# A routed feed-forward's bias b1: added by a matmul on TensorE instead of copied to all partitions and added on VectorE

## The chip, the cores and the metric

One core of one Trainium2 chip. The metric is the time of one execution on the device in microseconds (us), as the median of several runs. Beside it stands one execution taken by the hardware profiler.

## The reference

One layer of an encoder over 512 tokens and 16 meta tokens of width 1024: an mLSTM branch and a latent attention branch, mixed by gates, and then a mixture of experts. The change lies in the last:

```python
def moe(x, w_router, b_router, w1, b1, w2, b2):
    logits = (xt @ w_router) + b_router
    top_val, top_idx = lax.top_k(logits, 4)          # 4 of 32 experts
    gates = jax.nn.softmax(top_val, axis=-1)
    ...
    def expert_block(args):
        toks, wts, e = args
        hid = x_pad[toks] @ w1[e] + b1[e]             # w1: 1024 x 2048, b1: 2048, f32
        glu = jnp.minimum(hid[..., :1024], 7.0)
        lin = jnp.clip(hid[..., 1024:], -7.0, 7.0)
        act = glu * jax.nn.sigmoid(1.702 * glu) * (lin + 1)
        return (act @ w2[e] + b2[e]) * wts[:, None]   # w2: 1024 x 1024
```

The outputs are summed for each token, added to the residual, and normalised.

## The kernel before

The five engines run programs of their own, joined by semaphores. The stages follow one another: projections and the mLSTM (TensorE's loop at line 1221, one pair of heads an iteration), attention (line 1269), gates and output projection (line 1324, until some 900 us), the router (to some 970), and then 32 experts, the larger part of the time.

An expert has room for 96 tokens, three tiles of 32. Its tokens' rows are gathered from DRAM by POOL, turned by TensorE (`turn_x`) and copied by ACT to `xgT`. `up` multiplies them by w1: for each of 8 chunks of 128 rows, 3 tiles by 4 quarters make 12 matmuls of 128x32 weights and 512 columns. Quarter j of the output goes to partitions 32 j to 32 j + 31 of PSUM bank t, so four matmuls work in four column groups of the array. DVE (`activate`) adds b1, clamps, and forms the activation with ACT's sigmoid; `turn_act` turns it, and `down` multiplies it by w2, 8 x 12 matmuls of 256 columns. POOL adds the rows to the result in DRAM.

TensorE's order is written out in `step(e)`: up of expert e, with turn_act(e - 1) and turn_x(e + 1) before its fifth chunk, then down of expert e - 1. Its loop (line 1436) holds two steps an iteration and has 15 iterations; expert 0's up, and the products with b2 (line 1433), stand ahead of it, and the last step and the last down behind it. The waits of a step are those of `step` and `up_start` (lines 1380 and 363), and one for each chunk (line 1387, with its value from line 1384).

The weights have 12 places of 1 MB in `ring`. SP's queue loads each again for the next expert as soon as TensorE has used it (`load_up`, `load_down`), so a chunk is loaded about one expert ahead of its use. The expert's row of b1 is copied to the partitions by four DMAs of 64 KB behind chunk 0, in two buffers in turn.

Of the kernel before, what the change touches and what calls it, by code (L numbers as in the profile page):

```python
# [50 lines left out]

K_ID, K_ONE, K_MF, K_MB, K_US, K_IO, K_EPS, K_HALF, K_QTR, K_END = 0, 128, 256, 384, 512, 640, 672, 673, 674, 676


def constant_tables():

    c = np.zeros((P, K_END), np.float32)
    s, t = np.arange(P)[:, None], np.arange(P)[None, :]
    c[:, K_ID:K_ID + P] = s == t
    c[:, K_ONE:K_ONE + P] = 1  # L60
    c[:, K_MF:K_MF + P] = np.where(s <= t, 0.0, NEG)
    c[:, K_MB:K_MB + P] = np.where(s >= t, 0.0, NEG)
    c[:, K_US:K_US + P] = s < t
    c[:, K_IO:K_IO + E] = np.arange(E)
    c[:, K_EPS] = EPS
    c[:, K_HALF] = -0.5
    c[:, K_QTR] = np.arange(P) // 32
    half = ROPE // 2
    freqs = np.float32(10000.0) ** (-np.arange(half, dtype=np.float32) / np.float32(half))
    pos = np.concatenate([np.arange(META, TK), np.arange(META)]).astype(np.float32)  # L70
    ang = (pos[None, :] * freqs.astype(np.float32)[:, None]).astype(np.float32)
    cos, sin = np.cos(ang).astype(np.float32), np.sin(ang).astype(np.float32)
    rope = np.stack([np.tile(cos, (4, 1)), np.concatenate([-sin, sin, -sin, sin])], 1)
    pair = np.zeros((P, MT, TOPK, 2), np.float32)
    pair[:, :, :, 0] = (np.arange(P)[:, None] + P * np.arange(MT)[None, :])[:, :, None]
    spare = np.zeros((32, NQ, E, 2), np.float32)
    spare[:, :, :, 0] = T + np.arange(32)[:, None, None] + 32 * (np.arange(NQ) % TT)[None, :, None]
    return {"c_table": c, "c_rope": np.ascontiguousarray(rope), "c_pair": pair.reshape(P, -1),
            "c_spare": spare.reshape(32, -1)}
# [36 lines left out]
def build(ctx, nc, x, meta, norm_mix, w_in, m_b_i, m_b_f, m_norm, w_m_proj, w_uq, w_ukv, a_norm_q,  # L116
# [48 lines left out]
    def col(*dims):  # L165
# [58 lines left out]
    w_r_sb = sb("w_r_sb", KT * E)  # L224
    b1_sb = sb("b1_sb", 4 * QR)
    b1_bc = [view(b1_sb, n * 2 * QR, 2, QR) for n in range(2)]
    ints = sb("ints", 192, I32)
# [14 lines left out]
    zeros_ready, spare_zeroed = sem("zeros_ready"), sem("spare_zeroed")  # L242
    gains_in, wr_in, xt_ready, xt_stored, pe_xt, xtT_ready, pe_lg = map(sem, (
        "gains_in", "wr_in", "xt_ready", "xt_stored", "pe_xt", "xtT_ready", "pe_lg"))
    ex_in, ex_ready, sel_ready, pe_pos, rows_ready, table_ready, spare_in, placed, tab_in, idx4_ready = map(sem, (
        "ex_in", "ex_ready", "sel_ready", "pe_pos", "rows_ready", "table_ready", "spare_in", "placed", "tab_in", "idx4_ready"))
    g_all_ready, pe_gT, gT_ready, pe_b2, b2_added, acc_in = map(sem, ("g_all_ready", "pe_gT", "gT_ready", "pe_b2", "b2_added", "acc_in"))
    chunk_in = [sem(f"chunk_in{c}") for c in range(SLOTS)]
    xg_in, y_out, b1_in = [[sem(f"{name}{n}") for n in range(2)] for name in ("xg_in", "y_out", "b1_in")]
    idx_ready, pe_tx, xgT_ready, w1_used, w2_used, pe_hid, hid_used = map(sem, (  # L250
# [91 lines left out]
    l_sb = view(low_sb, 0, TT, QR)  # L342
    b1_cols = b1.rearrange("e (c j n) -> e c j n", c=2, j=4)
    CHUNK_SLOT = [0, 1, 2, 3, 8, 9, 10, 11, 4, 5, 6, 7]
# [28 lines left out]
    def _(sp):  # L373
# [60 lines left out]

        def load_b1(n, e):

            for j in range(4):
                sp.dma_start(b1_bc[n][32 * j:32 * j + 32], b1_cols[bass.ds(e, 1), :, j, :].rearrange("e c n -> (e c) n").partition_broadcast(32)).then_inc(b1_in[n], 16)

        def load_up(i, n, e):  # L440

            for k in range(KT):
                if k < KT - 1:
                    sp.wait_ge(w1_used, i * (KT - 1) + (k + 2 - KT))
                else:
                    sp.wait_ge(pe_hid, i)
                load_w1(k, e)
                if k == 0:
                    load_b1(n, e)

# [9 lines left out]
        for k in range(KT):  # L460
            load_w1(k, 0)
        load_b1(0, 0)
        sp.wait_ge(pe_h, 2 * MT)
        for c in range(4):
            load_w2(c, 0)
        load_up(1, 1, 1)
        with sp.Fori(1, E // 2) as i:
            for n in range(2):
                load_up(i * 2 + n, n, i * 2 + n)
                load_down(i * 2 + (n - 1), i * 2 + (n - 1))  # L470
        load_down(E - 1, E - 1)
        over = overflow(sp)
        with sp.If(over > 0):
            with sp.Fori(0, over) as n:
                sp.wait_ge(y_out[0], n * 48 + 24 * E)
                expert = sp.value_load(over_i[0:1, bass.ds(n, 1)], min_val=0, max_val=E - 1)
                first = sp.value_load(over_i[0:1, bass.ds(n + OVW, 1)], min_val=0, max_val=NQ - TT)
                for j in range(4):
                    sp.dma_start(tab_ov[32 * j:32 * j + 32], tab_by[:, bass.ds(first, TT), bass.ds(expert, 1), :].rearrange("p q e v -> p q (e v)")).then_inc(tabo_in, 16)
                load_up(n + E, 0, expert)  # L480
                load_down(n + E, expert)
# [11 lines left out]
    def _(pool):  # L493
# [69 lines left out]
        pool.dma_start(tab_by.rearrange("p q e v -> p (q e v)"), c_spare).then_inc(spare_in, 16)  # L563
        pool.wait_ge(ao_ready, H + 1)
        pool.dma_start(b2_sb[0:E, :], b2).then_inc(wr_in, 16)
        for m in range(MT):
# [85 lines left out]
    def _(act):  # L652
# [129 lines left out]
        def y_rows(e, n, stored):  # L782
# [3 lines left out]
            nc.scalar.copy(y_sb[n], PS[:, 3:3 + TT, 0:QR]).then_inc(y_ready, 1)  # L786

        act.sem_inc(y_ready, 1)
        turned_x(0, 0)
        turned_x(1, 1)  # L790
# [4 lines left out]
        for e in range(2):  # L795
            turned_act(e)
            turned_x(e + 2, e)
            sigmoid(e + 1)
            y_rows(e, e, None)
        with act.Fori(1, E // 2 - 1) as i:  # L800
            for n in range(2):
                turned_act(i * 2 + n)
                turned_x(i * 2 + (2 + n), n)
                sigmoid(i * 2 + (1 + n))
                y_rows(i * 2 + n, n, i * 48)
# [6 lines left out]
        with act.If(over > 0):  # L812
            with act.Fori(0, over) as n:
                turned_x(n + E, 0)
                sigmoid(n + E)
                turned_act(n + E)
                y_rows(n + E, 0, n * 48 + 24 * E)
# [6 lines left out]
    def _(dve):  # L824
# [305 lines left out]

        def activate(e, n, biases, gates):
            st = Steps(dve, expert_steps, e * 3)
            bias = [b1_bc[n][:, c, :].unsqueeze(1).broadcast_to([P, TT, QR]) for c in range(2)]
            dve.wait_ge(b1_in[n], biases)
            dve.wait_ge(pe_hid, e + 1)
            st.did(V.tensor_tensor(g_sb, PS[:, 0:TT, 0:QR], bias[0], ALU.add))  # L1136
            V.tensor_tensor(l_sb, PS[:, 0:TT, QR:2 * QR], bias[1], ALU.add).then_inc(hid_used, 1)
            st.settle()
            V.tensor_scalar(g_sb, g_sb, 7.0, None, ALU.min).then_inc(g_ready, 1)  # L1139
            dve.wait_ge(hid_used, e + 1)  # L1140
            st.alone(V.tensor_scalar(l_sb, l_sb, -7.0, 7.0, ALU.max, ALU.min))
            dve.wait_ge(g_ready, e + 1)
# [5 lines left out]

        activate(0, 0, 64, lambda t: tab[:, t, 0, 1:2])
        for m in range(MT):  # L1150
            dve.wait_ge(pe_b2, m + 1)
            b = 3 + 2 * (m % 2)
            V.tensor_tensor(xs[:, m, :], xs[:, m, :], PS[:, b:b + 2, :].rearrange("p a b -> p (a b)"), ALU.add).then_inc(b2_added, 1)
        activate(1, 1, 64, lambda t: tab[:, t, 1, 1:2])
        with dve.Fori(1, E // 2) as i:
            for n in range(2):
                activate(i * 2 + n, n, i * 64 + 64, lambda t: tab[:, t, bass.ds(i * 2 + n, 1), 1])
        over = overflow(dve)
        with dve.If(over > 0):
            with dve.Fori(0, over) as n:  # L1160
                dve.wait_ge(tabo_in, n * 64 + 64)
                V.tensor_scalar(idx_ov, tab_ov[:, :, 0], 4.0, ct[:, K_QTR:K_QTR + 1], ALU.mult, ALU.add).then_inc(idx_ov_ready, 1)
                activate(n + E, 0, n * 64 + (32 * E + 64), lambda t: tab_ov[:, t, 1:2])

# [5 lines left out]
    def _(pe):  # L1170
# [207 lines left out]

        def up_start(e):
            pe.wait_ge(xgT_ready, e * 2 + 2)  # L1380
            passed(pe)

        def up(e, n, k):
            pe.wait_ge(chunk_in[k], e * 16 + 16)
            for t in range(TT):
                for j in range(4):
                    last = nc.tensor.matmul(PS[32 * j:32 * j + 32, t, :].rearrange("p (c n) -> p c n", c=2), xgT[n][:, k, 32 * t:32 * t + 32],  # L1387
                                            w1_c[k][:, :, j * QR:(j + 1) * QR], start=k == 0, stop=k == KT - 1)
            last.then_inc(pe_hid if k == KT - 1 else w1_used, 1)
# [16 lines left out]
        def step(e, n, gathers):  # L1406

            pe.wait_ge(hid_used, e)
            up_start(e)
            for k in range(KT):  # L1410
# [10 lines left out]
        turn_x(0, 0, 48)  # L1421
        up_start(0)
        for k in range(KT):
# [19 lines left out]
        with pe.If(over > 0):  # L1443
            with pe.Fori(0, over) as n:
                pe.wait_ge(y_ready, n + (E + 1))
                pe.wait_ge(hid_used, n + E)
                turn_x(n + E, 0, n * 48 + (24 * E + 48))
                up_start(n + E)
                for k in range(KT):
# [24 lines left out]
```

## Time and profile before

| | us |
|---|---|
| median of 3 runs | 2201.04 |
| the runs | 2199.01, 2201.04, 2213.47 |
| the profiled execution | 2208.45 |
| its span in the profile | 2206.7 |
| TensorE busy (matmul) | 1975.7 |
| VectorE, ScalarE, GpSimd busy | 444.3, 267.3, 331.8 |

The span is the time from the first to the last instruction that the profiler recorded; 1.75 us of the profiled execution lie around it. PE is TensorE's matmul and PEld its loading of weights, PEldq its sequencer; DVE is VectorE, ACT ScalarE, POOL GpSimd, SP SyncE. "Issue" is time in which an engine waited for nothing that the profile shows.

### The profile page before, as it was taken

To read this page: it belongs to the slowest core of one execution; us is meant where nothing else is said; L and a number is where in the kernel's file an instruction comes from. 1 tells how busy PE (TensorE), PEld (TensorE's weight loads), DVE (VectorE), ACT (ScalarE), POOL (GpSimd) and SP (SyncE) were. 2 spreads that over 40 slices of the span, in tenths; PEclk is the share of its full clock that TensorE was granted. 3 is DMA by queue.
4 is the path that set the end of the run, shared out by engine and by line. 5 is a ranking of instruction groups with operands and counts; after the bars stand their busy time and mean duration, and the time that the engine had idled before them with its cause. 6 is when DMAs were issued, how large, how long until landed. Compare 5 with 4: busy or idle time off the path is not lost.

```text
span 2206.7 us, 36817 instructions
## 1 busy us (share of the span) xinstructions
PE 1975.7 (90%) x15441; PEld 900.2 (41%) x15441; DVE 444.3 (20%) x899; ACT 267.3 (12%) x531; POOL 331.8 (15%) x387
## 2 busy tenths in 40 slices
PE   7898999899999999839898889888988998899894
PEld 5454555444444444513343334333333333343342
DVE  3333433433310000222010111001110101010111
ACT  2202201122210000100010001000000000100001
POOL 3000000000000000150212121222112221212112
PEclk8989999999999999868999999999999999999997
DMA  3302111002032224327999999999999999999995
GB/s 106 94 23 76 57 35 34 12 12 56 0 109 77 77 78 180 115 100 306 360 390 342 368 360 384 349 361 379 370 365 348 386 352 363 357 393 334 370 331 168
DMA packets 163598, 495.08 MB, mean 224 GB/s; under 512 B 16048, under 2 KB 88848, under 8 KB 130656
## 3 DMA queue, kind: packets, MB, share of 16 engines
q1 hardware_dynamic: 112064, 442.83, 52.6%
q0 software_dynamic: 21600, 32.83, 6.7%
q10 hardware_dynamic: 29776, 16.91, 2.7%
q8 instruction: 148, 2.42, 0.4%
q14 instruction: 10, 0.08, 0.0%
HBM read 472.71 MB, written 19.96 MB: 223 GB/s over the span
## 4 chain that ended last, share of the span: by engine, by line
PE 88%; issue 6%; DVE 2%; DMA 2%; POOL 2%; ACT 1%; SPq 0%; POOLq 0%; DVEq 0%; ACTq 0%
PE PS L357 35%; PE PS L1387 32%; PE PS L1399 15%; PE PS L1243 1%; PE PS L1376 1%; PE PS L1369 1%; DMA ring<-in_w_in 1%; PE PS L1320 1%; POOL tab_dram L579 1%; PE PS L1433 0%; DVE ring L959 0%; DMA x_sb<-acc_dram 0%; ACT at_sb L707 0%; PE PS L1345 0%; POOL small L542 0%
## 5 line engine op out<-in xcount | busy, mean ns | idle before, releaser
L1387 PE MATMUL PS<-ring,mix_sb 128*32 128x512 f32 x6144 | 721.9, 614 | 94.9 <-issue 92.4
L1387 PEld LDWEIGHTS PS<-ring,mix_sb 128*32 128x32 f32 x6144 | 200.2, 112 | 577.5 <-issue 574.7
L1399 PE MATMUL PS<-ring,hm_sb 128*32 128x256 f32 x6144 | 337.4, 379 | 0.9 <-ACT hm_sb L775 0.9
L357 PE MATMUL PS<-uT_sb,ring 128*128 128x512 f32 (+1 forms) x736 | 298.0, 561 | 6.5 <-DMA ring<-in_w_in 3.5
L1399 PEld LDWEIGHTS PS<-ring,hm_sb 128*32 128x32 f32 x6144 | 199.6, 110 | 146.0 <-issue 18.5
L1136 DVE TENSOR_TENSOR hm_sb<-PS,b_sb 128x768 f32<-128x768 f32 x32 | 30.6, 957 | 1019.5 <-PE PS L1387 1019.5
L357 PEld LDWEIGHTS PS<-uT_sb,ring 128*128 128x128 f32 x736 | 140.1, 209 | 158.6 <-issue 154.7
L598 POOL DMA_INDIRECT acc_dram<-hm_sb,ints x96 | 152.0, 1583 | 47.3 <-POOL ints L617 24.0
L357 PE MATMUL PS<-ring 128*128 128x129 f32 (+4 forms) x592 | 145.7, 377 | 6.8 <-DVE ring L1009 3.5
L617 POOL COPY ints<-ints 128x3 int32 (+1 forms) x32 | 5.9, 185 | 857.4 <-ACT hm_sb L786 857.4
L357 PEld LDWEIGHTS PS<-ring 128*128 128x128 f32 (+1 forms) x592 | 83.1, 193 | 65.4 <-issue 52.0
L592 POOL DMA_INDIRECT mix_sb<-xt_dram,ints x96 | 94.7, 986 | 47.2 <-POOL ints L606 24.9
L357 PE MATMUL PS<-low_sb,ring 64*128 64x512 f32 (+1 forms) x224 | 87.7, 503 | 7.3 <-DVE hm_sb L836 4.6
L775 ACT COPY hm_sb<-PS 128x384 f32<-128x384 f32 x64 | 28.9, 481 | 467.5 <-PE PS L1376 437.8
L780 ACT ACTIVATE hm_sb<-hm_sb 128x768 f32<-128x768 f32 x32 | 27.1, 847 | 376.5 <-DVE hm_sb L1139 376.5
L357 PE MATMUL PS<-ring,uT_sb 128*128 128x256 f32 (+1 forms) x320 | 70.5, 380 | 0.0
L357 PEld LDWEIGHTS PS<-ring,uT_sb 128*128 128x128 f32 (+1 forms) x320 | 54.2, 171 | 14.4 <-issue 1.3
L357 PEld LDWEIGHTS PS<-low_sb,ring 64*128 64x128 f32 (+1 forms) x224 | 37.1, 191 | 55.9 <-issue 49.9
L1369 PE MATMUL PS<-ct,mix_sb 128*128 128x128 f32 x192 | 26.9, 278 | 35.2 <-DMA mix_sb<-xt_dram,ints 35.2
L357 PE MATMUL PS<-ring,mix_sb 128*128 128x512 f32 x128 | 55.2, 593 | 1.6 <-DVE mix_sb L1040 1.6
L357 PE MATMUL PS<-hm_sb,ring 128*128 128x512 f32 x128 | 56.2, 592 | 0.0
L357 PE MATMUL PS<-at_sb,ring 128*128 128x512 f32 x128 | 56.2, 592 | 0.0
(240 smaller groups left out, 1114.6 us busy)
## 6 DMA issues: line engine op xcount, KB each, us to landing
ring<-in_w SPq DMA_DIRECT2D x384, 1024.0 KB, 7.9
ring<-in_w_in SPq DMA_DIRECT2D x8, 1024.0 KB, 5.2
b_sb<-in_b SPq DMA_DIRECT2D x128, 64.0 KB, 4.8
ring<-in_w_in ACTq DMA_DIRECT2D x14, 512.0 KB, 4.0
ring<-in_w_in SPq DMA_DIRECT2D x10, 512.0 KB, 5.2
ring<-m_dram POOLq DMA_DIRECT2D x16, 256.0 KB, 4.5
ring<-in_w_out SPq DMA_DIRECT2D x1, 4096.0 KB, 13.9
ring<-in_w_m_proj ACTq DMA_DIRECT2D x7, 512.0 KB, 3.8
```

The lines of the kernel that those rows point to most:

```text
L357: last = nc.tensor.matmul(out, w, r, start=n == 0, stop=n == len(pairs) - 1)
L579: pool.indirect_dma_start(out=tab_dram, out_offset=bass.IndirectOffsetOnAxis(ap=drow_i[:, n:n + 1], axis=0), in_=pair[:, m, k, :], in_offs ...
L592: pool.indirect_dma_start(out=xg[n][:, t, :], out_offset=None, in_=xt_dram, in_offset=bass.IndirectOffsetOnAxis(ap=idx[:, t:t + 1], axis=0 ...
L598: pool.indirect_dma_start(out=acc_dram, out_offset=bass.IndirectOffsetOnAxis(ap=idx[:, t:t + 1], axis=0), in_=y_sb[n][:, t, :], in_offset= ...
L775: nc.scalar.copy(actT.rearrange("p (j h) (t c) -> p h t j c", h=2, t=TT)[:, h], bank(6 + h)[:, 0:TT * P].rearrange("p (t j c) -> p t j c", ...
L780: nc.scalar.activation(s_sb, g_sb, ACT.Sigmoid, scale=1.702).then_inc(s_ready, 1)
L1136: st.did(V.tensor_tensor(g_sb, PS[:, 0:TT, 0:QR], bias[0], ALU.add))
L1243: nc.tensor.matmul(PS[0:r, 5 + n % 2, :], kT[h0:h0 + DQK, j * P:j * P + r], qT[h0:h0 + DQK, :], start=True, stop=True).then_inc(pe_s, 1)
L1320: nc.tensor.transpose(PS[:, 4 + k % 2, j * P:(j + 1) * P], pr[:, k % 3, j * P:(j + 1) * P], ident)
L1369: last = nc.tensor.transpose(PS[:, 3 + h, t * P:(t + 1) * P], xg[n][:, t, h * P:(h + 1) * P], ident)
L1387: last = nc.tensor.matmul(PS[32 * j:32 * j + 32, t, :].rearrange("p (c n) -> p c n", c=2), xgT[n][:, k, 32 * t:32 * t + 32], w1_c[k][:, :, ...
L1399: last = nc.tensor.matmul(PS[32 * j:32 * j + 32, 3 + t, 0:QR], actT[:, k, 32 * t:32 * t + 32], w2_c[k // 2][:, k % 2, j * QR:(j + 1) * QR] ...
```

## The change

b1 is loaded once, as 32 rows of 2048 f32, and POOL splits it into three bf16 parts whose sum is b1 to about 24 bits: the value rounded, the rest rounded, and the rest of that. They are held in `b1_part`, expert e's parts in partitions e, 32 + e and 64 + e; partitions 96 to 127 are zero. For each expert ACT copies one column of the constants, which is one in those three partitions and zero in the others, to a 128x32 bf16 tile, `b1_sel`. Before the first chunk of an expert TensorE multiplies it by `b1_part`: twelve matmuls over all 128 rows, which leave b1's row in each of the output's rows, and the chunks are added to that. DVE's adds are gone, and the two clamps read PSUM. The four DMAs an expert, their buffers and their semaphores are gone; SP's and DVE's loops now take one expert an iteration.

```diff
-K_ID, K_ONE, K_MF, K_MB, K_US, K_IO, K_EPS, K_HALF, K_QTR, K_END = 0, 128, 256, 384, 512, 640, 672, 673, 674, 676
+K_ID, K_ONE, K_MF, K_MB, K_US, K_IO, K_EPS, K_HALF, K_QTR, K_SEL, K_END = 0, 128, 256, 384, 512, 640, 672, 673, 674, 676, 708
...
+    c[0:96, K_SEL:K_SEL + E] = np.arange(96)[:, None] % 32 == np.arange(E)
...
-    b1_sb = sb("b1_sb", 4 * QR)
-    b1_bc = [view(b1_sb, n * 2 * QR, 2, QR) for n in range(2)]
+    b1_part = sb("b1_part", 2 * FF, BF16)
+    b1_low = sb("b1_low", 2 * FF, BF16, E)
+    b1_sel = [sb(f"b1_sel{n}", 32, BF16) for n in range(2)]
...
-    b1_cols = b1.rearrange("e (c j n) -> e c j n", c=2, j=4)
+    b1_f = view(low_sb, 0, 2 * FF)
+    b1_by = b1_part.rearrange("p (c n) -> p c n", c=2)
...
-        def load_b1(n, e):
-
-            for j in range(4):
-                sp.dma_start(b1_bc[n][32 * j:32 * j + 32], b1_cols[bass.ds(e, 1), :, j, :].rearrange("e c n -> (e c) n").partition_broadcast(32)).then_inc(b1_in[n], 16)
-
-        def load_up(i, n, e):
+        def load_up(i, e):
...
                 load_w1(k, e)
-                if k == 0:
-                    load_b1(n, e)
...
         pool.wait_ge(ao_ready, H + 1)
+        pool.dma_start(b1_f[0:E, :], b1).then_inc(b1f_in, 16)
+        st.alone(nc.gpsimd.memset(b1_part[:, :], 0.0))
+        pool.wait_ge(b1f_in, 16)
+        for n in range(3):
+            st.alone(nc.gpsimd.tensor_copy(b1_low[:, :], b1_f[0:E, :]))
+            nc.gpsimd.tensor_copy(b1_part[32 * n:32 * n + E, :], b1_low[:, :]).then_inc(b1_ready, 1)
+            if n < 2:
+                st.alone(nc.gpsimd.tensor_tensor(b1_f[0:E, :], b1_f[0:E, :], b1_low[:, :], ALU.subtract))
+        pool.wait_ge(b1_ready, 3)
         pool.dma_start(b2_sb[0:E, :], b2).then_inc(wr_in, 16)
...
+        def select(n, column):
+
+            nc.scalar.copy(b1_sel[n][:, :], column.broadcast_to([P, 32])).then_inc(b1_selected, 1)
+
         act.sem_inc(y_ready, 1)
+        for e in range(2):
+            select(e, ct[:, K_SEL + e:K_SEL + e + 1])
...
                 turned_x(i * 2 + (2 + n), n)
+                select(n, ct[:, bass.ds(i * 2 + (K_SEL + 2 + n), 1)])
                 sigmoid(i * 2 + (1 + n))
...
-        def activate(e, n, biases, gates):
-            st = Steps(dve, expert_steps, e * 3)
-            bias = [b1_bc[n][:, c, :].unsqueeze(1).broadcast_to([P, TT, QR]) for c in range(2)]
-            dve.wait_ge(b1_in[n], biases)
+        def activate(e, gates):
+            st = Steps(dve, expert_steps, e)
             dve.wait_ge(pe_hid, e + 1)
-            st.did(V.tensor_tensor(g_sb, PS[:, 0:TT, 0:QR], bias[0], ALU.add))
-            V.tensor_tensor(l_sb, PS[:, 0:TT, QR:2 * QR], bias[1], ALU.add).then_inc(hid_used, 1)
-            st.settle()
-            V.tensor_scalar(g_sb, g_sb, 7.0, None, ALU.min).then_inc(g_ready, 1)
+            V.tensor_scalar(g_sb, PS[:, 0:TT, 0:QR], 7.0, None, ALU.min).then_inc(g_ready, 1)
+            V.tensor_scalar(l_sb, PS[:, 0:TT, QR:2 * QR], -7.0, 7.0, ALU.max, ALU.min).then_inc(hid_used, 1)
             dve.wait_ge(hid_used, e + 1)
-            st.alone(V.tensor_scalar(l_sb, l_sb, -7.0, 7.0, ALU.max, ALU.min))
...
-        def up_start(e):
+        def up_start(e, n):
             pe.wait_ge(xgT_ready, e * 2 + 2)
+            pe.wait_ge(b1_selected, e + 1)
             passed(pe)
+            for t in range(TT):
+                for j in range(4):
+                    nc.tensor.matmul(PS[32 * j:32 * j + 32, t, :].rearrange("p (c n) -> p c n", c=2), b1_sel[n][:, :],
+                                     b1_by[:, :, j * QR:(j + 1) * QR], start=True, stop=False)
 
         def up(e, n, k):
             pe.wait_ge(chunk_in[k], e * 16 + 16)
             for t in range(TT):
                 for j in range(4):
                     last = nc.tensor.matmul(PS[32 * j:32 * j + 32, t, :].rearrange("p (c n) -> p c n", c=2), xgT[n][:, k, 32 * t:32 * t + 32],
-                                            w1_c[k][:, :, j * QR:(j + 1) * QR], start=k == 0, stop=k == KT - 1)
+                                            w1_c[k][:, :, j * QR:(j + 1) * QR], start=False, stop=k == KT - 1)
             last.then_inc(pe_hid if k == KT - 1 else w1_used, 1)
...
         turn_x(0, 0, 48)
-        up_start(0)
+        pe.wait_ge(b1_ready, 3)
+        up_start(0, 0)
```

## Rows read from the trace of the kernel before

**Rows 1.** The profile page, first part: busy us, share of the span, instructions.
```profile
PE 1975.7 (90%) x15441; PEld 900.2 (41%) x15441; DVE 444.3 (20%) x899; ACT 267.3 (12%) x531; POOL 331.8 (15%) x387
```

**Rows 2.** Chain of waits, expert loop: start us, us, what.
```profile
1598.18 10.36 PE PS L1399 x192
1608.55 5.54 issue
1614.09 3.63 PE PS L1387 x12
1617.72 0.54 issue
1618.25 9.71 PE PS L1387 x84
...
1650.22 10.30 PE PS L1387 x96
...
1661.98 10.44 PE PS L1387 x96
...
1682.78 5.46 issue
...
1691.86 1.29 issue
1693.15 11.50 PE PS L1387 x84
```

**Rows 3.** TensorE's sequencer, branches of two loops: ns min/median/max, first, last start.
```profile
L1436 PEldq COMPARE_BRANCH  x15: 83/6182/6352, 1082.1 to 2133.9; - x15
L1221 PEldq COMPARE_BRANCH  x4: 76/214/240, 174.4 to 410.0; - x4
```

**Rows 4.** DMA, one iteration of the expert loop; engines there and in mLSTM.
```profile
q8 instruction: 9, 0.15, 0.8%
ring<-in_w SPq DMA_DIRECT2D x24, 1024.0 KB, 8.1
b_sb<-in_b SPq DMA_DIRECT2D x8, 64.0 KB, 5.3
1613.40:1687.70 74.30, 68.15 (x792) 27.39 (x792) 9.98 (x16) 6.73 (x12) 16.26 (x17) 0.96 1.00 366
178.00:253.00 75.00, 69.68 (x279) 41.86 (x278) 28.11 (x74) 14.25 (x38) 3.45 (x6) 1.00 0.16 48
```

**Rows 5.** Timeline of TensorE's weight loads behind the branch: start, us, what.
```profile
1614.08 0.20 PEld L1387 LDWEIGHTS PS<-ring,mix_sb 128*32 128x32 f32 x8 [6.02 <-issue]
1614.94 0.19 PEld L1387 LDWEIGHTS PS<-ring,mix_sb 128*32 128x32 f32 x2 [0.65 <-issue]
1615.79 0.19 PEld L1387 LDWEIGHTS PS<-ring,mix_sb 128*32 128x32 f32 x2 [0.67 <-issue]
```

**Rows 6.** TensorE's sequencer at the top of a step, lines 1380, 363, 1384.
```profile
L1380 PEldq FUSED_REGOPS  x30: 37/37/37, 1014.9 to 2101.3; - x30
L363 PEldq EVENT_SEMAPHORE  x40: 51/51/51, 128.0 to 2134.0; - x40
L1384 PEldq FUSED_REGOPS  x30: 37/37/37, 1015.2 to 2101.6; - x30
```

**Rows 7.** The profile page, costliest groups: matmuls of the up phase.
```profile
L1387 PE MATMUL PS<-ring,mix_sb 128*32 128x512 f32 x6144 | 721.9, 614 | 94.9 <-issue 92.4
```

**Rows 8.** Chain of waits behind expert 0: start, us, what.
```profile
1001.64 0.47 DVE hm_sb L1139
```

**Rows 9.** POOL's groups: during the gates, and at the kernel's start.
```profile
L568 POOL TENSOR_SCALAR small<-small 128x1 f32<-128x1 f32 x2 | 0.4, 185 | 250.0 <-ACT uT_sb L753 250.0
L518 POOL COPY ring<-ring 128x512 f32<-128x512 f32 x2 | 1.7, 840 | 0.0
```

**Rows 10.** Engines, granted clock, DMA share: two stretches behind the branch.
```profile
1611.70:1618.30 6.60, 3.67 (x16) 0.62 (x19) 0.00 (x0) 0.00 (x0) 5.04 (x5) 0.50 1.02 314
1618.50:1627.00 8.50, 8.50 (x82) 2.34 (x76) 0.00 (x0) 0.00 (x0) 1.91 (x2) 1.00 0.87 238
```

More of the change, by code:

```diff
@@ L242, in build @@
     zeros_ready, spare_zeroed = sem("zeros_ready"), sem("spare_zeroed")
-    gains_in, wr_in, xt_ready, xt_stored, pe_xt, xtT_ready, pe_lg = map(sem, (
-        "gains_in", "wr_in", "xt_ready", "xt_stored", "pe_xt", "xtT_ready", "pe_lg"))
+    gains_in, wr_in, b1f_in, b1_ready, b1_selected, xt_ready, xt_stored, pe_xt, xtT_ready, pe_lg = map(sem, (
+        "gains_in", "wr_in", "b1f_in", "b1_ready", "b1_selected", "xt_ready", "xt_stored", "pe_xt", "xtT_ready", "pe_lg"))
     ex_in, ex_ready, sel_ready, pe_pos, rows_ready, table_ready, spare_in, placed, tab_in, idx4_ready = map(sem, (
@@ L248, in build @@
     chunk_in = [sem(f"chunk_in{c}") for c in range(SLOTS)]
-    xg_in, y_out, b1_in = [[sem(f"{name}{n}") for n in range(2)] for name in ("xg_in", "y_out", "b1_in")]
+    xg_in, y_out = [[sem(f"{name}{n}") for n in range(2)] for name in ("xg_in", "y_out")]
     idx_ready, pe_tx, xgT_ready, w1_used, w2_used, pe_hid, hid_used = map(sem, (
@@ L461, in _ @@
             load_w1(k, 0)
-        load_b1(0, 0)
         sp.wait_ge(pe_h, 2 * MT)
@@ L465, in _ @@
             load_w2(c, 0)
[L466 to L470, printed above, removed]
+        load_up(1, 1)
+        with sp.Fori(2, E) as i:
+            load_up(i, i)
+            load_down(i - 1, i - 1)
         load_down(E - 1, E - 1)
@@ L479, in _ @@
                     sp.dma_start(tab_ov[32 * j:32 * j + 32], tab_by[:, bass.ds(first, TT), bass.ds(expert, 1), :].rearrange("p q e v -> p q (e v)")).then_inc(tabo_in, 16)
-                load_up(n + E, 0, expert)
+                load_up(n + E, expert)
                 load_down(n + E, expert)
@@ L797, in _ @@
             turned_x(e + 2, e)
+            select(e, ct[:, K_SEL + e + 2:K_SEL + e + 3])
             sigmoid(e + 1)
@@ L813, in _ @@
             with act.Fori(0, over) as n:
+                act.wait_ge(pe_hid, n + E)
+                select(0, ct[:, bass.ds(act.value_load(over_i[0:1, bass.ds(n, 1)], min_val=0, max_val=E - 1) + K_SEL, 1)])
                 turned_x(n + E, 0)
@@ L1147, in activate @@
             dve.wait_ge(act_ready, e * TT + TT)
-        activate(0, 0, 64, lambda t: tab[:, t, 0, 1:2])
+        activate(0, lambda t: tab[:, t, 0, 1:2])
         for m in range(MT):
@@ L1153, in _ @@
             V.tensor_tensor(xs[:, m, :], xs[:, m, :], PS[:, b:b + 2, :].rearrange("p a b -> p (a b)"), ALU.add).then_inc(b2_added, 1)
[L1154 to L1157, printed above, removed]
+        with dve.Fori(1, E) as i:
+            activate(i, lambda t: tab[:, t, bass.ds(i, 1), 1])
         over = overflow(dve)
@@ L1162, in _ @@
                 V.tensor_scalar(idx_ov, tab_ov[:, :, 0], 4.0, ct[:, K_QTR:K_QTR + 1], ALU.mult, ALU.add).then_inc(idx_ov_ready, 1)
-                activate(n + E, 0, n * 64 + (32 * E + 64), lambda t: tab_ov[:, t, 1:2])
+                activate(n + E, lambda t: tab_ov[:, t, 1:2])
         for m in range(MT):
@@ L1408, in step @@
             pe.wait_ge(hid_used, e)
-            up_start(e)
+            up_start(e, n)
             for k in range(KT):
@@ L1447, in _ @@
                 turn_x(n + E, 0, n * 48 + (24 * E + 48))
-                up_start(n + E)
+                up_start(n + E, 0)
                 for k in range(KT):
```

## The prediction

> **What bounds the kernel now.** I read the page first: TensorE is busy for 90% of the span [rows 1]. Then the chain of waits inside the expert loop, since all the edits but a few lie there. In it the reader sees TensorE alone: nothing else ends last from one expert to the next. One step (up of one expert, the turns, down of the expert before) runs from 1650.22 to 1682.78, 32.56 us, without a gap [rows 2]. Two steps make one iteration of TensorE's loop, and an iteration takes 1682.78 - 1608.55 = 74.23 us, so 74.23 - 2 x 32.56 = 9.1 us of each are lost, all at its beginning: 5.54 us of "issue", twelve matmul records at a slow pace (3.63 us), another 0.54 us of "issue", and then the remaining 84 at full pace [rows 2].
>
> What is that wait? No engine or DMA releases it. The loop's own branch (line 1436) takes 6.18 us at the median where the branch that closes the mLSTM loop (line 1221) takes 0.21 [rows 3]. During one iteration the instruction queue q8 moves nine packets of 16 KB; during a mLSTM iteration, of 279 + 278 recorded instructions, the answer on DMA has no row of q8 at all [rows 4]. So the small loop stays in TensorE's instruction memory and the expert loop does not: it is fetched anew each time round, and at the branch TensorE waits for the block of code that holds the loop's top. The second gap is the same thing again. Before it TensorE ran the loop's header and exactly twelve LDWEIGHTS (8 + 2 + 2) and twelve MATMUL [rows 2, 5], then nothing until 1618.25: the block ended there, and the next had been asked for only when the first was entered. The header is four instructions, lines 1436, 1380, 363 and 1384 [rows 3, 6], so the edge of a block lies 4 + 24 = 28 instructions behind the loop's top.
>
> DMA's share of busy time is 1.00 in the loop [rows 4], but a weight chunk lands 8.1 us after its issue [rows 4] and is wanted a whole step later, so no wait for a chunk is in the chain.
>
> **The change part by part.** The sum is made against the profiled execution, 2208.45 us, which is 7.4 above the median of the three runs; I carry the difference over to the median, 2201.04.
>
> Twelve bf16 matmuls an expert, 128x32 weights, 512 columns. The trace has no bf16. A record of the down phase, 256 columns of f32, costs 10.36 / 192 = 0.054 us at the pace of the chain; one of the up phase, 512 columns, 10.44 / 96 = 0.109 [rows 2, 7]. [...] I take 0.054, so 12 x 0.054 = 0.65 us an expert, 20.7 in all; the other end is the full up record, 1.3 an expert, 41.7. Nothing hides it: TensorE sets the end.
>
> The adds taken from DVE (lines 1136, 1137). The two clamps now read PSUM and take the adds' places, so lines 1139 and 1141 go, 0.47 us each. In the loop a whole down phase, 10.4 us, covers this chain, so it is worth nothing there. Once, behind expert 0, DVE's chain is the one that ends last [rows 8]: 0.9 us off. The bank is released as late as before.
>
> The copies of b1 (four 64 KB DMAs an expert, SP's queue). They are 8 x 64 KB of an iteration's 27.21 MB, some 2% [rows 4], stand in SP's queue between chunk 0 and chunk 1, and no chunk is waited for: nothing, except that fetches of code may come a little sooner.
>
> The new work on the others. ACT's two selects an iteration lie behind the turned copies of the expert before, and TensorE asks for them a step later. POOL's preparation (a 256 KB load, a memset, six copies and two subtractions of 2048 columns) is bounded by the 128x512 copy of 0.84 us, four times that being 3.4, and twice as much for the two subtractions: some 35 us; POOL has 250 us idle there [rows 9]. If that cover were missing it would be 35 us once.
>
> [...]
>
> [...]
>
> **The rivals.**
> [...]
>
> *B. Code placement doesn't matter:* the gaps stay 5.5 and 0.5 us with matmuls between them, because the code ahead is padded or the block isn't bound to a place. Then only the matmuls are paid: 20.7 - 0.9 = +20, 2221 us. For it: twelve records run before the second gap at every branch, which a time (not a place) could also cause. Against it: twelve exactly, while the gap behind them varies, 0.54 and 1.29 us [rows 2].
>
> *C. The bf16 matmuls don't overlap in the four column groups* as f32 does, or changing type between records costs: 0.65 us becomes 1.3 to 2.6 an expert. With my case that is 2275 to 2315.
>
> *D. Lighter DMA gives back what the matmuls cost*, through quicker fetches: at most about 1 us for each of two fetches and 14 branches, 28 us; with B's 20 that is 2195 to 2215.
>
> **How the numbers follow.** My case 0.55; A 0.13 kept and 0.04 not kept; B 0.16; D 0.05; C 0.07. The range must hold 8 in 10: from 2208 (most of D, all of B, the low end of my case, 2226) to 2285 (my case with its bounds, the nearer part of C). Left out is A, the far part of C and some of D. A difference of 1% (22 us) is about what a measurement of this kernel can tell from none: faster than 2179 is A kept, 0.13; within are B, D and A not kept, 0.25; slower the rest, 0.62.
>
> **What would show it.** In the profile after: the branch of line 1436 still some 6 us, q8 some nine packets an iteration; after it, header instructions only, a second wait of 4 to 5 us without a matmul between, so one "issue" of 9 to 10 us in the chain; then twelve bf16 records, at half clock, in about 1.3 us; in the second step of an iteration twelve in 0.65. An iteration is 74.23 + 0.65 + 3.0 = 78 us. The prediction is wrong if bf16 matmuls ran before the second gap (B), if the branch took 0.2 us (A), or if DVE, POOL or ACT ended a wait of TensorE's in the loop.

## The result, and the profile after

The changed kernel takes 2248.64 us, the median of 4 runs (2243.97 to 2252.77), where the kernel before takes 2202.74 (2199.01 to 2213.47, 4 runs). The ratio is 1.0187, 95% interval 1.0166 to 1.0208: 1.9% slower. The profiled execution of after took 2245.88 us, 37.4 more than that of before.

The chain of waits of after, one iteration of the expert loop (start, us, what):

```profile
1619.62 10.36 PE PS L1410 x192
1629.98 8.40 issue
1638.38 1.47 PE PS L1391 x12
1639.85 11.09 PE PS L1398 x96
...
1673.20 0.65 PE PS L1391 x12
1673.85 10.30 PE PS L1398 x96
...
1706.40 8.42 issue
```

Here the 5.54 us of "issue", the twelve records and the second gap of [rows 2] have become a single wait of 8.4 us, and behind it come the bf16 matmuls (line 1391) and all 96 f32 records. In the second step of the iteration the bf16 matmuls take 0.65 us. TensorE's sequencer at this branch (ns min/median/max, first and last start):

```profile
L1448 PEldq COMPARE_BRANCH  x15: 83/6078/6212, 1083.9 to 2169.4; - x15
L1386 PEldq FUSED_REGOPS  x1: 37/37/37, 1634.9 to 1634.9; - x1
L1387 PEldq ALU_OP  x1: 36/36/36, 1635.0 to 1635.0; - x1
L366 PEldq EVENT_SEMAPHORE  x1: 51/51/51, 1638.3 to 1638.3; - x1
```

The last three are from 1630 to 1640 us only. The branch (line 1448) still takes 6.08 us [rows 3]. Then the loop's first instruction (line 1448, at 1634.8) and the two of lines 1386 and 1387 run, three in all, and the fourth, line 366, comes 3.3 us later. So the edge of a block is three instructions behind the loop's top; the experiments test this reading. The branch's first and last start also give the length of 14 iterations: 2169.4 - 1083.9 = 1085.5 us, where it was 2133.9 - 1082.1 = 1051.8 [rows 3]. Of the 37.5 us by which the span grew 33.7 lie there, 2.4 an iteration.

The clock and the DMA of after (engines' busy us, PEclk, DMA share, GB/s), and the DMA of an iteration:

```profile
1638.30:1641.00 2.70, 2.62 (x20) 0.96 (x24) 0.00 (x0) 0.00 (x0) 2.02 (x2) 0.50 0.52 97
1641.00:1644.00 3.00, 3.00 (x32) 0.86 (x28) 0.00 (x0) 0.00 (x0) 0.95 (x1) 0.95 0.33 90
1628.60:1705.00 76.40, 68.00 (x824) 28.15 (x820) 8.12 (x12) 6.76 (x14) 16.19 (x16) 0.96 0.94 352
```

```profile
q8 instruction: 10, 0.16, 0.9%
ring<-in_w SPq DMA_DIRECT2D x24, 1024.0 KB, 6.9
```

The granted clock is 0.50 in the first stretch, where TensorE takes up work, and 0.95 on the mean of the next, where before had 0.50 and 1.00 [rows 10]. Code is still fetched in each iteration (q8, ten packets in this stretch and 126 in the 14 iterations, as in before). One packet of q8 moves from 1635 to 1636 us, behind the loop's first instruction at 1634.8, the next from 1639 to 1640, behind the fourth at 1638.3; in before one moves from 1615 to 1616, behind the first weight load at 1614.1 [rows 5], and none from there to 1619. So in both a block's successor moved only once the block was entered, as the prediction reads it. The two packets ahead of these move from 1609 to 1611 us in before and from 1628 to 1629 and 1632 to 1633 in after: further apart, as its (3) says. Ahead of the loop after has what was counted: twelve loads and twelve matmuls of line 1391 between 970 and 984 us, and one EVENT_SEMAPHORE more, at 976.2 (line 1387). A weight chunk lands 6.9 us after its issue where it took 8.1 [rows 4]. What was expected to be hidden is: POOL's memset, casts, copies and subtractions together take 21.2 us, and behind them POOL is idle for another 222.5.

```profile
L566 POOL TENSOR_TENSOR low_sb<-low_sb,b_low 32x2048 f32<-32x2048 f32 x2 | 8.1, 4057 | 0.1
L571 POOL TENSOR_SCALAR small<-small 128x1 f32<-128x1 f32 x2 | 0.4, 188 | 222.5 <-ACT uT_sb L756 222.5
```

### The profile page after: what moved, and what is told of

Same layout as the page of the kernel before. It is cut to its first block, busy times and chain, and to the rows that moved or that the text cites. A ratio compares the mean times of both kernels' runs of the same rounds, so it can differ in the third digit from the quotient of the medians.

```text
span 2244.2 us, 37217 instructions
## 1 busy us (share of the span) xinstructions
PE 1983.0 (88%) x15825; PEld 914.7 (41%) x15825; DVE 414.5 (18%) x835; ACT 267.8 (12%) x564; POOL 352.8 (16%) x397
## 4 chain that ended last, share of the span: by engine, by line
PE 87%; issue 7%; DVE 2%; DMA 2%; POOL 1%; ACT 1%; SPq 0%; POOLq 0%; DVEq 0%; ACTq 0%
PE PS L360 35%; PE PS L1398 31%; PE PS L1410 15%; PE PS L1391 2%; PE PS L1249 1%; PE PS L1382 1%; PE PS L1375 1%; DMA ring<-in_w_in 1%; PE PS L1326 1%; POOL tab_dram L582 1%; PE PS L1445 0%; DMA x_sb<-acc_dram 0%; DVE ring L972 0%; ACT at_sb L710 0%; POOL small L536 0%
## 5 line engine op out<-in xcount | busy, mean ns | idle before, releaser
L1398 PE MATMUL PS<-ring,mix_sb 128*32 128x512 f32 x6144 | 696.2, 610 | 0.0
L1147 DVE TENSOR_SCALAR hm_sb<-PS 128x768 f32<-128x768 f32 x32 | 30.7, 958 | 1082.1 <-PE PS L1398 1082.1
L1391 PE MATMUL PS<-b_part,b_sel 128*32 128x512 bf16 x384 | 36.8, 501 | 125.2 <-issue 123.4
L1391 PEld LDWEIGHTS PS<-b_part,b_sel 128*32 128x32 bf16 x384 | 11.2, 109 | 141.9 <-issue 137.4
L789 ACT COPY hm_sb<-PS 128x768 f32<-128x768 f32 x32 | 25.6, 799 | 276.0 <-PE PS L1410 276.0
```

What stands on the lines that cost most here:

```text
L1147: V.tensor_scalar(g_sb, PS[:, 0:TT, 0:QR], 7.0, None, ALU.min).then_inc(g_ready, 1)
```

## The experiments

Each was measured beside the kernel before on the same chip, and its ratio is to that. The median of the kernel before was 2209.09 us beside the first four experiments of the table (after_pad2 to before_pad28), 2207.42 beside the next four and 2208.74 beside the last four; the row "before" has the 2202.74 of the change itself. Idle instructions are increments of a semaphore that nobody waits for, put on TensorE's queue in its idle time ahead of the experts (behind the router's logits, or, for the long ones, behind the transposes of the gates):

```diff
+        for _ in range(N):
+            pe.sem_inc(waits_passed, 1)
```

| kernel | us | ratio to before, 95% | branch, us | 14 iterations, us |
|---|---|---|---|---|
| before | 2202.74 | 1 | 6.18 | 1051.8 |
| after | 2248.64 | 1.0187 (1.0166 to 1.0208) | 6.08 | 1085.5 |
| after_pad2 | 2243.67 | 1.0144 (1.0117 to 1.0171) | 6.09 | 1087.7 |
| after_pad3 | 2087.85 | 0.9452 (0.9437 to 0.9468) | 0.21 | 929.7 |
| before_pad25 | 2246.53 | 1.0151 (1.0116 to 1.0186) | 6.04 | 1085.4 |
| before_pad28 | 2136.85 | 0.9698 (0.9651 to 0.9745) | 0.21 | 972.0 |
| after_pad3_copies | 2129.19 | 0.9663 (0.9626 to 0.9700) | 0.21 | 963.0 |
| after_pad3_double | 2103.32 | 0.9524 (0.9495 to 0.9554) | 0.21 | 947.9 |
| before_pad28_nocopies | 2070.74 | 0.9373 (0.9345 to 0.9402) | 0.21 | 912.9 |
| after_pad231 | 2236.36 | 1.0142 (1.0110 to 1.0175) | 6.07 | 1074.2 |
| after_copies | 2256.33 | 1.0215 (1.0200 to 1.0229) | 6.06 | 1098.3 |
| before_pad25_nocopies | 2232.21 | 1.0108 (1.0094 to 1.0122) | 6.07 | 1072.8 |
| after_pad139 | 2088.12 | 0.9445 (0.9425 to 0.9464) | 0.21 | 929.7 |
| after_pad144 | 2120.95 | 0.9594 (0.9549 to 0.9640) | 0.21, four over 7 | 964.2 |

The last two columns are of the one profiled execution of each kernel: the median of the branch's time, and the difference of its first and last start. The four runs of a kernel lie 1.5 (after_pad3) to 29 us apart (after_pad144; 22 in before_pad28, 18 in before_pad25), so a difference of a few us between two kernels is within the noise, unless the traces show where it arises.

**Two and three idle instructions in the changed kernel.** N = 2 and N = 3.

> The changed kernel with two idle instructions (increments of a semaphore that nobody waits for) ahead of TensorE's expert loop. The theory of places says that the block's edge, three instructions behind the loop's top, is now one behind it: still no matmul ahead of it, the branch still 6 us, nine fetches an iteration, and the time is that of the changed kernel, 2249 us (2243 to 2256). The rival, that only what runs counts and not where it stands, expects 2249 too; this run is the control for the next one.

> The changed kernel with three idle instructions ahead of the loop. The theory of places: the loop now begins exactly on a block's edge and touches seven blocks instead of eight; with one fetched ahead that is eight, the loop stays in instruction memory, the branch takes 0.2 us, no fetches in the loop, and 14 x 11 to 12 us are gone: 2249 - 160 = about 2090 us. If the loop is fetched anew all the same, only the second wait goes: about 2215 us. The rival (places don't matter) expects 2249 us, as for two.

The counts of blocks here and below take 256 instructions for a block, which after_pad231, further on, bears out. The loop has some 1605 instructions in before (792 + 792 records [rows 4] and some twenty of the sequencer's) and 1654 in the changed kernel.

2243.67 and 2087.85 us: one instruction that does nothing is worth 156 us. The branches of the two (ns min/median/max):

```profile
L1450 PEldq COMPARE_BRANCH  x15: 83/6092/6192, 1083.7 to 2171.4; - x15
```
```profile
L1450 PEldq COMPARE_BRANCH  x15: 76/208/221, 1081.8 to 2011.5; - x15
```

The slow time of the loop is a matter of place, and the edge is where the prediction put it, to the instruction. In the chain of waits of after_pad3 there is now no gap at all:

```profile
1504.46 10.36 PE PS L1412 x192
1514.82 0.65 PE PS L1393 x12
1515.47 10.30 PE PS L1400 x96
...
1537.67 10.36 PE PS L1412 x192
1548.03 0.65 PE PS L1393 x12
```

An expert takes 1548.03 - 1514.82 = 33.21 us, and 33.21 - 0.65 is the 32.56 of the prediction.

**The same places in the kernel before.** N = 25 and N = 28, and nothing else of the change.

> The kernel before with 25 idle instructions ahead of the loop, as many as the change puts there, and nothing else of it. The theory of places: the edge is three behind the loop's top, the branch is followed by a wait of some 3.2 us without a matmul between, and the time rises by the change's rise less its matmuls: 46 - 20 = 26, so 2229 us (2218 to 2240). The rival, that the change costs its matmuls and a slower loop of some other cause (ACT's selects, POOL, PSUM), expects 2203 us.

> The kernel before with 28 idle instructions ahead of the loop. The theory of places: the loop begins on an edge, 1605 instructions touch seven blocks, nothing is fetched in the loop, and the 9 to 10 us lost in each of 14 iterations are gone: about 2203 - 135 = 2068 us (2060 to 2085). The rival expects 2203 us.

2246.53 us with 25, above the expected 2218 to 2240: as much as the changed kernel takes. Its chain of waits shows one wait without a matmul in it, 1.7 us longer than that of after (9.9 us against 8.8 on the mean of the 14 branches), and behind it the 96 records in 11.81 us (granted clock 0.50 to 1648.0, then 0.81 to 1650.0) where they take 10.3 at a clock of 1.00:

```profile
1625.58 10.36 PE PS L1401 x192
1635.94 10.13 issue
1646.07 11.81 PE PS L1389 x96
```

With 28 it came to 2136.85, much faster, but not the 2068 expected. The branch takes 0.21 us, so the code stays; what is late now is the weights. TensorE's waits in the expert part (us in all, times, longest), the DMA from 1100 to 2000 us, and the engines from 1500 to 1600 of before_pad28:

```profile
PE PS L1389 <- DMA ring<-in_w: 37.8, 65, 1.0
ring<-in_w SPq DMA_DIRECT2D x308, 1024.0 KB, 25.3
b_sb<-in_b SPq DMA_DIRECT2D x101, 64.0 KB, 14.9
1500.00:1600.00 100.00, 95.11 (x1144) 38.71 (x1140) 14.98 (x24) 9.81 (x18) 19.42 (x20) 1.00 1.04 383
```

and the same of after_pad3, which moves more and waits for none of it:

```profile
ring<-in_w SPq DMA_DIRECT2D x325, 1024.0 KB, 8.7
1500.00:1600.00 100.00, 100.00 (x1232) 42.18 (x1228) 12.17 (x18) 10.14 (x21) 24.34 (x24) 1.00 1.03 402
```

A chunk lands 25.3 us after its issue, not 8.7. The first part of the theory held, "TensorE alone sets the end" did not once the gaps were gone. The starts of the branch tell when: the first three iterations take (1278.5 - 1083.2) / 3 = 65.1 us, TensorE's own pace, and from 1419.2 us on one takes (2055.2 - 1419.2) / 9 = 70.7, or 35.3 an expert. The loads begin with a lead, and lose it. In that part (1500 to 1925 us) SP's queue never waits for TensorE to give back a place, as it does without the copies (after_pad3: 335.6 us in 154 waits); its own DMA instructions become long instead. Those of w2 from 1500 to 1925 us, in before_pad28 and in after_pad3:

```profile
L433 SPq DMA_DIRECT2D ring<-in_w x49: 383/4792/5392, 1498.3 to 1922.3; - x49
L436 SPq DMA_DIRECT2D ring<-in_w x52: 372/378/384, 1507.3 to 1913.5; - x52
```

**What holds it there: the copies?** One run puts them back into the changed kernel (`load_b1(e)` is the four DMAs, into a buffer that nobody reads), one takes them out of the kernel before (this one adds the rows of experts 0 and 1 to all later experts, and its VectorE no longer waits for a copy).

```diff
 after_pad3_copies
...
+                if k == 0 and copies:
+                    sp.wait_ge(b1_in, i * 64)
+                    load_b1(e)
```
```diff
 before_pad28_nocopies
-                if k == 0:
+                if k == 0 and isinstance(i, int) and i == 1:
                     load_b1(n, e)
...
-            dve.wait_ge(b1_in[n], biases)
+            dve.wait_ge(b1_in[n], 64)
```

> The changed kernel with three idle instructions ahead of the loop, so that no code is fetched in it, and with the four DMAs of b1 an expert put back into SP's queue, into a buffer that nobody reads. The theory that the copies are what holds the kernel before at 2137 us once its code is no longer fetched expects about 2137 us here too (2125 to 2155), with waits of TensorE for chunks. The rival, that VectorE's adds or the wait for the copies held it, expects 2088 us.

> The kernel before with 28 idle instructions ahead of the loop, and b1 copied for experts 0 and 1 alone; from expert 2 on VectorE adds the two rows that are already there, so the work of all engines but the copies is left as it is. If the copies alone hold it at 2137 us, TensorE sets the end: 2088 - 20.7 for the bf16 matmuls + 0.9 for VectorE's longer chain behind expert 0 = 2068 us (2062 to 2076). If something else holds it, 2137.

2129.19 and 2070.74 us. The copies cost 2129 - 2088 = 41 us in the one and 2137 - 2071 = 66 in the other, where no code is fetched in the loop. In after_pad3_copies TensorE waits for chunks again (line 1413, 17.7 us in 35 waits), and comes to the same pace: from 1481.3 us on an iteration takes (2044.5 - 1481.3) / 8 = 70.4 us, where after_pad3 takes 66.4. It comes to it later than before_pad28 and loses less by it, because the bf16 matmuls make TensorE itself slower, 66.4 against 65.1; hence 41 against 66. VectorE's adds, still there in before_pad28_nocopies, cost nothing: its 14 iterations take 65.2 us each.

**The price of the matmuls.** The twelve are done twice, in up_start of every expert but 0.

```diff
+            for again in range(times):
...
-                                     b1_by[:, :, j * QR:(j + 1) * QR], start=True, stop=False)
+                                         b1_by[:, :, j * QR:(j + 1) * QR], start=True, stop=again < times - 1)
```

> The changed kernel with three idle instructions ahead of the loop, and the twelve bf16 matmuls of each expert but the first done twice, the second time from the start, so the result is the same. The theory prices them at 0.65 us an expert with nothing to hide them: 2088 + 31 x 0.65 = 2108 us (2105 to 2112). If they were hidden, 2088; if they kept each other waiting, more than 2115.

2103.32 us (2098.05 to 2108.47), 15.5 more by the medians and a little below the expected 2105 to 2112. The chain of waits prices them directly (24 records in 1.29 us), and 14 iterations took 947.9 instead of 929.7 us, 18.2 = 28 x 0.65:

```profile
1525.56 1.29 PE PS L1394 x24
```

**The change with the edge where it was.** N = 231; 25 + 231 is one block of 256, if a block has so many.

> The changed kernel with 231 idle instructions in TensorE's idle time ahead of the experts; with the change's own 25 that is one whole block of 256, so the edge lies 28 behind the loop's top again, as in the kernel before. The theory: the 12 bf16 matmuls run between the two waits in place of 12 f32 records of twice their length, so an iteration costs 0.65 in its second step and 1.3 in its first, less some 1.1 for quicker fetches: 2203 + 14 x 0.85 + 3 - 1 = 2217 us (2205 to 2226). That the change is nothing but the place would give 2203, that place is nothing and the matmuls are paid, 2249.

2236.36 us, above the expectation and below 2249. Its chain of waits:

```profile
1619.74 5.16 issue
1624.90 1.47 PE PS L1393 x12
1626.37 1.95 issue
1628.32 13.34 PE PS L1400 x96
```

The twelve bf16 matmuls, 24 instructions, run between the two waits at each of the 14 branches, where twelve f32 records ran before [rows 2, 5]. So 256 instructions are a whole number of blocks, and since the loop's 1605 or 1654 instructions come in 126 / 14 = 9 packets an iteration, where blocks of half the size would take 13 or more, they are one block. What I had left out is the clock: it was 0.50 from 1628.3 to 1634.0 us, and the 96 records behind the wait take 13.34 us here and 11.98 at the next branch, not 10.3. The loop took 22.4 us longer than before's, but only 1085.5 - 1074.2 = 11.3 less than that of after (12 by the medians). The place that costs the kernel before 33.6 us costs the changed one 11.

**The other two corners.** Copies or none, matmuls or none, with the edge three instructions behind the loop's top; the edits are those above.

> The changed kernel, its loop's edge where the change puts it, with the four DMAs of b1 an expert put back into SP's queue, into a buffer that nobody reads. The kernel before with 25 idle instructions takes as long as the changed one though it has no bf16 matmuls. If the copies are why, by slower fetches of code at the branch, then both together give 2249 + 17 = 2266 us (2258 to 2276). If the copies cost nothing while code is fetched, 2249.

> The kernel before with 25 idle instructions ahead of the loop, and b1 copied for experts 0 and 1 alone; from expert 2 on VectorE adds the two rows that are already there. The fourth corner: neither copies nor matmuls, edge three behind the loop's top. If the copies cost some 17 us there and the matmuls 20.7: 2229 us (2221 to 2236). If the copies cost nothing there, 2247.

2256.33 us, below its expected 2258 to 2276, and 2232.21. By the 14 iterations of the profiled executions: neither 1072.8, copies 1085.4, matmuls 1085.5, both 1098.3. Each adds 12.6 to 12.9 us, with the other or without it. By the medians the copies cost 14 us without the matmuls and 8 with them, and the matmuls 16 and 10; that the four figures of the traces agree so closely is more than runs with this spread can promise. The copies' part is mostly wait for code: "issue" ahead of the up phase falls from 138.5 us in before_pad25 to 128.7 without them, and from 135.7 in after_copies to 122.8 in after, 0.7 to 0.9 a branch.

**How far a loop can reach.** N = 139 and N = 144 in the changed kernel.

> The changed kernel with 139 idle instructions in TensorE's idle time ahead of the experts: the loop begins 136 instructions behind an edge, and 136 + 1654 = 1790, two short of seven blocks. If what counts is the number of blocks that the loop touches, seven and one ahead, it stays in instruction memory: 2088 us (2084 to 2094), branch 0.2 us. If only a loop that begins on the edge is kept, some 2200.

> The same with 144 idle instructions: 141 + 1654 = 1795, three instructions into the eighth block. By the count of blocks the loop is fetched anew: the branch takes 6 us; the block at the loop's top holds 115 instructions, so the next one is asked for in time and there is no second wait. 2088 + 14 x (5.5 of wait + 2 of slow clock) = 2193 us (2180 to 2215). If it is not the count of blocks, 2088 as with 139.

With 139 it took 2088.12 us and fetched nothing: a loop that begins in the middle of a block is kept as well, if it ends within the seventh. With 144 I expected a fetch at every branch. There were four among 14 (7.06 to 7.34 us each), the others took 0.2, and the runs spread from 2103 to 2132 us:

```profile
L1450 PEldq COMPARE_BRANCH  x15: 76/211/7337, 1081.2 to 2045.4; - x15
PE PS L1393 <- issue: 25.1, 4, 6.4
```

The last three instructions of the loop are in the eighth block there. The queue q8 moved 36 packets during the 14 iterations, 4 x 9. Why the code was fetched at four branches and not at the other ten, no run shows.

## Why the prediction was right, and where its sum was not

The forecast was 2253 us and the measurement is 2249. Part of this nearness is luck: the sum said +52, the medians say +46, and the profiled executions, against which it was made, +37. By steps:

- *The loop's wait is a fetch of code, and the change moves the edge from 28 to 3 instructions behind its top.* Right, to the instruction (three header instructions, then the wait), and shown by after_pad2 against after_pad3 and by before_pad25 and before_pad28. The second wait itself was 3.3 us, not 4 to 5, so the "issue" was 8.4 where 9 to 10 was said.
- *The price of the place,* 18.3 + 18.2 - 4 = 32.5 us in 14 branches. Before_pad25 has the place and nothing else: 1085.4 - 1051.8 = 33.6. The terms hold there one by one. The time from TensorE's last record to its first one behind the last wait was 92.4 us of "issue" and 14 x 3.6 of records, 142.8, in before and is 138.5, so -4; and what the records behind it take beyond the full pace went from 1.0 to 2.4 us a branch. The term of 18.2 us, 1.3 a branch for slower records behind the wait, was my estimate, and no run shows it as such; what the runs showed in its place is this +1.4, with the granted clock at 0.50 for the first 1.9 us behind the wait and at 0.81 on the mean of the next 2 (before_pad25, from 1646.1 us).
- *In the changed kernel* that term holds too (2.3 us a branch), but the time until the second block is there is 122.8 us and not 138.5: the term of -4 was -20. Where the 16 us come from the four corners say: 10 to 13 are the copies, 3 to 6 the matmuls.
- *The bf16 matmuls,* 0.65 us an expert, 20.7 in all. The 0.054 us a record was my estimate; after shows 0.65 / 12 = 0.054 us, where an f32 record of the same 512 columns takes 10.30 / 96 = 0.107, and the doubled matmuls say 0.65 an expert too. In the loop of the changed kernel they cost 1085.5 - 1072.8 = 12.7 instead of 28 x 0.65 = 18.2, since the waits for code are 5.9 us shorter with them (122.8 against 128.7); why is open.
- *The copies: "nothing, except that fetches of code may come a little sooner".* This is the term that was mis-sized. They were worth 12.8 us of the loop. With the edge three behind the loop's top the matmuls and the copies cancel, so the changed kernel takes as long there as the kernel before (1085.5 and 1085.4). That does not make the place the whole of the change: with the edge at 28 the change still costs 22.4 us of the loop, and the place adds 11.3. Which part is put down to which depends on the order in which they are taken. No run has the edge at 28 with neither copies nor matmuls, so what each costs there is open. Rival D named the mechanism, at up to 28 us, but I gave it no share of the likeliest case.
- *DVE's 0.9 us once.* The chain behind expert 0 has lost the two pieces of 0.47 us [rows 8], and TensorE's wait for it there went from 2.9 to 1.9 us; too small to test by the time.
- *POOL and ACT.* Hidden, as said: POOL's work took 21 us where 35 were said, with 222 idle behind it, and ACT's two casts of 0.25 us an iteration are in no chain.

Rival A did not come about by a margin of three instructions; made to come about, it gave 2088 us where 2094 was written. B is excluded by the idle instructions, C by the 0.65 us in the chain.

The view of the bound was incomplete in one respect. A DMA share of 1.00 with chunks landing in 8 us I took as "not the bound". It was the next bound, hidden by TensorE's waits for code: with these gone the kernel before is held by its loads at 2137 us, and the change, slower by 1.9% as it stands, is then faster: 0.9452 / 0.9698 = 0.975 by the ratios, 2087.85 / 2136.85 = 0.977 by the medians. The version that beats both kernels is the changed one with three idle instructions, 2087.85 us, 5.5% below the kernel before; there TensorE has no gap left in the loop.

## What to carry to other kernels

When the chain of waits shows "issue" at the top of a long loop and nothing releases it, look at the branch's own duration (here 6.18 us against 0.21) and at the instruction queue of the DMA (here nine packets an iteration against none), and count instructions to the edge of the block: here the place alone cost the kernel before 33.6 us of the 14 iterations, and twelve bf16 matmuls an expert 18.2 (after_pad3_double). One idle instruction tests it (156 us between after_pad2 and after_pad3). Compare two versions of a kernel at more than one place of the loop's code: here the change is 1.9% slower as it stands, level with before at the same bad place, and 2.3 to 2.5% faster where neither fetches. A transfer that is hidden behind such a gap should be priced again for when the gap is gone: the copies cost 13 us of the 14 iterations with it, and 33 and 59 without.

## What was not expected of the hardware

- A loop of 1654 instructions of TensorE was kept where it touches seven blocks of 256 (after_pad3 and after_pad139: fetches in the loop: none, branch 0.21 us) and fetched anew, nine packets of 16 KB an iteration, one more than it touches, where it touches eight (after, after_pad2), for 11 us an iteration (1087.7 - 929.7 over 14).
- Three instructions into the eighth block (after_pad144) it was fetched anew at 4 branches of 14, of 7.06 to 7.34 us, and kept at the others, of 0.2.
- The copies of b1 are 1.9% of an iteration's bytes [rows 4], but with them an iteration that is held by the loads takes 70.4 to 70.7 us, and without them 65.2 is reached with 0.5 us of waits for chunks in all: at least 8% for 1.9%. DMA moved 383 GB/s with them (before_pad28, 1500 to 1600 us) and 402 without (after_pad3).
